# Long convolution by token residue modulo four, with part of its elementwise work on GpSimd

## The chip, the cores and the metric

One core of a Trainium2 chip runs the whole kernel, all in 32-bit floats. The metric is the device time of one execution in microseconds; the kernel before takes 4211.11 us (median of three runs, 4209.9 to 4212.46).

## What is computed

The reference is two transformer blocks over 1024 tokens of width 1024. The first block has a retention branch, a gated long convolution (the "hyena" branch) and a mixture of experts; the second has latent attention, a recurrent branch and another mixture of experts. Only the long convolution is touched. Cut to what matters:

```
zf = rfft(z, n=2048, axis=tokens)                       # z: 1024 tokens x 512 channels
hf = rfft(h_fwd, n=2048) + conj(rfft(h_bwd, n=2048))
y  = irfft(zf * hf, n=2048)[:1024] + z * skip
out = x0 * y                                            # x0, z, out: 1024 x 512
```

## The kernel before, in words

The program is a chain of phases. Each phase is a block with its own semaphores and one instruction list per engine, and the next phase begins on every engine only when all have left the last. SP issues most loads (the rows show its queue as SPq).

The transforms are products with tables of cosines and sines. Before the change the tokens are split into even and odd ones, 512 each, and a frequency and its mirror image share the work: with E the sum over even tokens and O the sum over odd ones, the two are E+O and E-O. So each table is 512x512, stored as 4 frequency tiles (`kt`) by 4 token tiles (`mt`) of 128x128. One product is 128x128 by 128 x 512 channels, 32-bit, and the trace shows it as two MATMUL records.

`phase_front` (L667) makes the two filters in K.X and loads frequency tiles 0 and 1 of the table `k_fwd` and the first tokens.

`phase_forward_norm` (L939) transforms the filters and at the same time normalises and transposes the tokens. VectorE first makes `he` and `ho`, the sum and the difference of the two filters (L1031, L1035). TensorE does 16 groups of four products, each followed by four 128x128 transposes of normalised tokens (L991, L998). ScalarE evicts half of the transposes (L1018) and the odd half of a pair of groups (L1023). VectorE evicts the other transposes (L1062) and forms H (L1068 to L1072).

`phase_taps` (L2005) projects, applies the short convolution and the gate, and transposes z into token order by residue (L2043, a source read at a step of two elements, 8 bytes). In its weight sums GpSimd works beside VectorE (L1936 to L1941). `Pairs` holds their code.

`phase_convolve` (L1075) does the convolution: for each of four frequency tiles 16 forward products (L1119), ScalarE's copies of the odd sums (L1148), and 20 VectorE operations of 128x512, each (L1156 to L1178): four butterflies, the complex product with H in two halves, four recombinations into K.X. Then come the inverse products (L1111), 64 in all, even tokens first, and for each of the 8 result banks VectorE adds the skip term (L1184) and multiplies with x0 (L1187), over every second token:

```
dve.scalar_tensor_tensor(odd[:, n % 2, :], split(xc[:, 4 + c, :], par), vec(K.cols, "hy_skip", c),
                         bk[n][:, :], ALU.mult, ALU.add).then_inc(skipped, 1)
dve.wait_ge(skipped, n + 1)
dve.tensor_tensor(split(hyT[:, c, :], par), odd[:, n % 2, :], split(xc[:, c, :], par), ALU.mult)
```

`Chain` issues an instruction and makes its engine wait until that one has finished. The order of every engine is written out by hand. The retention branch's first phase (`context`) follows.

Of the kernel before, what the change touches and what calls it, by code (L numbers as in the profile page):

```python
# [15 lines left out]
F32 = mybir.dt.float32  # L16
# [5 lines left out]
P = 128  # L22
D = 1024
KT = D // P
SEQ = 1024
# [630 lines left out]
def fwd_table(I, F, kt):  # L656

    return F.tab[:, kt % 2, :, :], I["k_fwd"][kt].rearrange("p (a n) -> p a n", n=P)
# [280 lines left out]
def phase_forward_norm(nc, I, K, fl, F, he, ho, H, src, outT, scale, shift):  # L939


    NT, XS, YS, FB = SEQ // P, 3, 3, 6
    with Mem(nc, "fwdnorm") as m:
        tab, x, full, xin = F.tab, F.x, F.full, F.xin
        odd = m.sb("odd", [P, 2, C])
        ys = m.sb("y", [P, YS, D])
        sq = m.sb("sq", [P, D])
        ss = m.sb("ss", [P, NT, 4])
        bk = m.banks(8)
        fb, nb = bk[0:FB], bk[FB:8]  # L950
        evac = m.sems("evac0", "evac1")
        hes, mm, copied, outs = m.sems("hes", "mm", "copied", "outs")
        summed, rooted, inv, yok, turned = m.sems("summed", "rooted", "inv", "yok", "turned")
        b = m.block()
        tok = lambda t: slice(t * P, (t + 1) * P)

        @b.sync
        def _(sp):
            def table(kt):

                if kt >= 2:
                    sp.wait_ge(mm, 4 * (kt - 1))
                sp.dma_start(tab[:, kt % 2, :, :], I["k_fwd"][kt].rearrange("p (a n) -> p a n", n=P)).then_inc(full[kt % 2], 16)

            def tokens(t):

                if t >= XS:
                    sp.wait_ge(yok, t - XS + 1)
                sp.dma_start(x[:, t % XS, :], src[tok(t), :]).then_inc(xin[t % XS], 16)

            tokens(3)
            tokens(4)
            table(2)
            tokens(5)
            tokens(6)
            table(3)
            tokens(7)

        @b.tensor
        def _(pe):  # L980
            for n in range(16):
                kt, a = divmod(n, 4)
                if a == 0:
                    pe.wait_ge(full[kt % 2], 16 * (kt // 2 + 1))
                if n >= FB:
                    pe.wait_ge(outs, (n - FB) // 2 + 1)
                part = (he, he, ho, ho)[a]
                if kt == 0:
                    pe.wait_ge(hes, 4 * (a + 1))
                for mt in range(4):  # L990
                    last = pe.matmul(fb[n % FB][:, :], tab[:, kt % 2, a * 4 + mt, :], part[:, (a % 2) * 4 + mt, :], start=(mt == 0), stop=(mt == 3))  # L991
                last.then_inc(mm, 1)
                t, h = divmod(n, 2)
                if h == 0:
                    pe.wait_ge(yok, t + 1)
                pe.wait_ge(evac[h], t + 1)
                for q in range(4):
                    last = pe.transpose(nb[h][:, q * P:(q + 1) * P], ys[:, t % YS, (4 * h + q) * P:(4 * h + q + 1) * P], K.ident[:, :])  # L998
                last.then_inc(turned, 1)

        @b.scalar
        def _(act):
# [12 lines left out]
            for t in range(NT):  # L1015
                act.wait_ge(turned, 2 * t + 1)
                for k in range(4):
                    last = act.activation(outT[:, k, tok(t)], nb[0][:, k * P:(k + 1) * P], ACT.Identity, scale=scale(k), bias=shift(k))  # L1018
                last.then_inc(evac[0], 1)
                act.wait_ge(mm, 2 * t + 2)  # L1020
                if t >= 2:
                    act.wait_ge(outs, t - 1)
                act.activation(odd[:, t % 2, :], fb[(2 * t + 1) % FB][:, :], ACT.Copy).then_inc(copied, 1)  # L1023
                if t + 2 < NT:
                    squares(t + 2)

        @b.vector
        def _(dve):
            def filt_he(t):

                dve.tensor_tensor(he[:, t, :], fl[:, t, 0:C], fl[:, t, C:2 * C], ALU.add).then_inc(hes, 1)  # L1031

            def filt_ho(t):

                dve.tensor_tensor(ho[:, t, :], fl[:, t, 0:C], fl[:, t, C:2 * C], ALU.subtract).then_inc(hes, 1)  # L1035
# [11 lines left out]
            for t in range(4):  # L1047
                filt_he(t)
            normed(0)
            for t in range(4, 8):  # L1050
                filt_he(t)
            normed(1)
            for t in range(4):
                filt_ho(t)
            for t in range(4, 8):
                filt_ho(t)
            for t in range(NT):
                if t + 2 < NT:
                    normed(t + 2)
                dve.wait_ge(turned, 2 * t + 2)  # L1060
                for k in range(4, 8):
                    last = dve.tensor_scalar(outT[:, k, tok(t)], nb[1][:, (k - 4) * P:(k - 3) * P], scale(k), shift(k), ALU.mult, ALU.add)  # L1062
                last.then_inc(evac[1], 1)
                kt, j = divmod(t, 2)
                dve.wait_ge(copied, t + 1)
                even = fb[2 * t % FB]
                if j == 0:
                    dve.tensor_tensor(H[:, kt, 0, :], even[:, :], odd[:, t % 2, :], ALU.add)  # L1068
                    dve.tensor_tensor(H[:, kt, 1, :], even[:, :], odd[:, t % 2, :], ALU.subtract).then_inc(outs, 1)
                else:  # L1070
                    dve.tensor_tensor(H[:, kt, 2, :], odd[:, t % 2, :], even[:, :], ALU.add)
                    dve.tensor_tensor(H[:, kt, 3, :], odd[:, t % 2, :], even[:, :], ALU.subtract).then_inc(outs, 1)  # L1072


def phase_convolve(nc, I, K, zn, H, prod, xc, hyT):  # L1075


    with Mem(nc, "conv") as m:
        tab = m.sb("tab", [P, 2, 16, P])
        odd = m.sb("odd", [P, 2, C])  # L1080
        z = m.sb("z", [P, 4, C])
        t = m.sb("t", [P, 4, C])
        y = hyT[:, :, 0:C]
        back = [[tab[:, a, :, :].rearrange("p (k b) n -> p k (b n)", b=4) for a in range(2)], [z[:, :, :], t[:, :, :]]]
        bk = m.banks(8)
        full = m.sems("full0", "full1")
        bfull = [m.sems("bfull00", "bfull01"), m.sems("bfull10", "bfull11")]
        mm, copied, outs, chain, turned, bmm, skipped = m.sems("mm", "copied", "outs", "chain", "turned", "bmm", "skipped")
        b = m.block()
        multiplied = lambda kt: 4 * (kt + 1)  # L1090

        @b.sync
        def _(sp):
            table = lambda par, a: I["k_inv"][par].rearrange("p (a n) -> p a n", n=C)[:, 4 * a:4 * a + 4, :]
            for kt in range(4):
                if kt >= 2:
                    sp.wait_ge(mm, 4 * (kt - 1))
                sp.dma_start(tab[:, kt % 2, :, :], I["k_fwd"][kt].rearrange("p (a n) -> p a n", n=P)).then_inc(full[kt % 2], 16)
            for a in range(2):
                sp.wait_ge(mm, 4 * (3 + a))  # L1100
                sp.dma_start(back[0][a], table(0, a)).then_inc(bfull[0][a], 16)
            sp.wait_ge(chain, multiplied(3))
            for a in range(2):
                sp.dma_start(back[1][a], table(1, a)).then_inc(bfull[1][a], 16)

        @b.tensor
        def _(pe):

            def inverse(par, c, a, kt, first, last):

                return pe.matmul(bk[4 * par + c][:, :], prod[:, kt, 2 * par + a, c * P:(c + 1) * P], back[par][a][:, kt, :], start=first, stop=last)  # L1111

            for kt in range(4):
                pe.wait_ge(full[kt % 2], 16 * (kt // 2 + 1))
                if kt >= 2:
                    pe.wait_ge(outs, kt - 1)
                for a in range(4):
                    for mt in range(4):
                        last = pe.matmul(bk[kt % 2 * 4 + a][:, :], tab[:, kt % 2, a * 4 + mt, :], zn[:, (a % 2) * 4 + mt, :],  # L1119
                                         start=(mt == 0), stop=(mt == 3))  # L1120
                    last.then_inc(mm, 1)
            pe.wait_ge(outs, 3)
            pe.wait_ge(chain, multiplied(2))
            for a in range(2):
                pe.wait_ge(bfull[0][a], 16)
                for c in range(4):
                    for kt in range(3):
                        inverse(0, c, a, kt, a == 0 and kt == 0, False)
            pe.wait_ge(chain, multiplied(3))
            for c in range(4):  # L1130
                inverse(0, c, 0, 3, False, False)
                inverse(0, c, 1, 3, False, True).then_inc(bmm, 1)
            for a in range(2):
                pe.wait_ge(bfull[1][a], 16)
            pe.wait_ge(outs, 4)
            for c in range(4):
                for n in range(8):
                    last = inverse(1, c, n // 4, n % 4, n == 0, n == 7)
                last.then_inc(bmm, 1)

        @b.scalar
        def _(act):
            for kt in range(4):
                for j in range(2):
                    act.wait_ge(mm, 4 * kt + (2 if j == 0 else 4))
                    if kt:
                        act.wait_ge(outs, kt)
# [2620 lines left out]
```

## Time and profile before

| | |
|---|---|
| median of three runs | 4211.11 us |
| span of the profiled execution, first to last instruction | 4218.0 us |
| TensorE busy | 3775.0 us, 89% |
| VectorE busy | 1511.3 us, 36% |
| ScalarE busy | 1024.2 us, 24% |
| GpSimd busy | 607.1 us, 14% |
| mean granted clock of TensorE | 0.961 of full speed |

The profile prints no other time of the profiled execution than its span, 6.9 us (0.16%) above the median. Times in rows count from the span's start. PE is TensorE's products, PEld its weight loads, DVE VectorE, ACT ScalarE, POOL GpSimd, SPq the DMA issues of SP. The arrow in brackets names what ended an idle time. A merged row ("x8") shows start and length of a run of equal instructions. The last record of a run of products overlaps the next instruction, so spacing is read from starts.

### The profile page before, as it was taken

The numbers are of one execution on the slowest core, as the hardware profiler recorded it, in microseconds if no ns is written. First come the engines' busy times: TensorE is split into PE (matmuls) and PEld (weight loads), VectorE is DVE, ScalarE is ACT, GpSimd is POOL, SyncE is SP. The second block draws the span as 40 slices with busy tenths as digits, with TensorE's granted clock in tenths as the row PEclk, the third lists the DMA queues.
The fourth block names the chain that finished last, engine by engine and source line by source line (L and its number), as shares of the span: only waits on it lengthen the run. The fifth ranks groups of instructions, "written<-read, shape, count | busy, mean of one in ns | idle before, by whom it ended". The sixth has DMA issues, their size and how long they took to land. (4 is left out here: it accounts for less than half of the span.)

```text
span 4218.0 us, 96770 instructions
## 1 busy us (share of the span) xinstructions
PE 3775.0 (89%) x42145; PEld 2433.0 (58%) x42145; DVE 1511.3 (36%) x2627; ACT 1024.2 (24%) x2394; POOL 607.1 (14%) x748
## 2 busy tenths in 40 slices
PE   7999899989999799999978999978888799996995
PEld 2444448864444488888854444457777544445774
DVE  5465235541212400000053666645556522222003
ACT  3201100131101122222242441034455211112333
POOL 1120000001000000000010001335555311000112
PEclk9999999999999799999989999989999999997998
DMA  8352332121112389999950001100000211306998
GB/s 296 131 166 80 131 90 80 60 55 35 35 35 104 148 337 389 394 394 397 400 186 15 9 2 45 45 2 4 4 4 4 78 35 52 101 35 244 385 386 313
DMA packets 243728, 601.68 MB, mean 143 GB/s; under 512 B 37593, under 2 KB 150008, under 8 KB 223515
## 3 DMA queue, kind: packets, MB, share of 16 engines
q1 hardware_dynamic: 200723, 471.21, 30.8%
q0 software_dynamic: 19120, 73.68, 5.1%
q10 hardware_dynamic: 23640, 53.20, 3.8%
q8 instruction: 194, 3.18, 0.3%
q14 instruction: 51, 0.42, 0.0%
HBM read 522.78 MB, written 71.05 MB: 141 GB/s over the span
## 5 line engine op out<-in xcount | busy, mean ns | idle before, releaser
L1752 PE MATMUL experts_bank<-experts_uT,ex_wu 128*64 128x96 f32 x9216 | 390.2, 247 | 26.9 <-PE experts_bank L1738 22.2
L1752 PEld LDWEIGHTS experts_bank<-experts_uT,ex_wu 128*64 128x64 f32 x9216 | 383.9, 137 | 43.6 <-issue 43.6
L1825 DVE TENSOR_TENSOR experts_hT<-experts_si,experts_bank 128x384 f32<-128x384 f32 (+1 forms) x68 | 31.3, 460 | 724.2 <-PE experts_bank L1752 724.2
L1752 PE MATMUL experts_bank<-experts_uT,b2z_hT 128*64 128x96 f32 x4096 | 178.4, 248 | 27.0 <-DMA b2z_hT<-in_w 17.8
L1752 PEld LDWEIGHTS experts_bank<-experts_uT,b2z_hT 128*64 128x64 f32 x4096 | 172.9, 138 | 41.6 <-issue 41.6
L1738 PE MATMUL experts_bank<-mixed_T,experts_hT 128*32 128x256 f32 (+1 forms) x2592 | 194.2, 451 | 0.0
L1738 PEld LDWEIGHTS experts_bank<-mixed_T,experts_hT 128*32 128x32 f32 x2592 | 111.1, 110 | 69.1
L1780 ACT ACTIVATE experts_uT<-experts_bank,all_modrun 128x96 f32<-128x96 f32 x296 | 99.3, 439 | 212.6 <-PE experts_bank L1733 212.6
L2401 POOL TENSOR_TENSOR b2z_hT<-b2z_hT,rwkv_level 128x256 f32<-128x256 f32 x192 | 140.8, 767 | 44.2 <-DVE b2z_hT L2880 34.0
L1361 DVE TENSOR_TENSOR merge_u<-merge_bank,merge_sg 128x512 f32<-128x512 f32 x16 | 11.1, 691 | 338.9 <-PE merge_bank L1294 338.9
L1718 POOL COPY experts_now<-ex_idx 96x1 int32 x68 | 12.5, 184 | 798.3 <-PE experts_bank L1733 788.5
L3282 PE MATMUL mh_sc<-mla_KTs,mh_QT 128*128 128x512 f32 x256 | 120.7, 594 | 5.9 <-ACT mla_KTs L3327 5.9
L1485 PE MATMUL route_bank<-ex_wu,mixed_T 128*128 128x512 f32 x256 | 114.3, 606 | 9.0 <-DMA ex_wu<-in_w_out 9.0
L1280 PE MATMUL merge_bank<-mix_qk,merge_w 128*128 128x512 f32 x256 | 114.9, 603 | 5.1 <-DMA merge_w<-in_ret_w_o 5.1
L2421 PE MATMUL rc_banks<-rc_xy,rc_p 64*64 64x64 f32 x2560 | 106.9, 220 | 8.3 <-issue 8.1
L485 PE MATMUL qk_bank<-mix_hT,all_X 128*128 128x512 f32 x256 | 110.1, 592 | 1.0 <-PEq L48 1.0
L3334 ACT ACTIVATE mh_pb<-mh_sc,mh_mx 128x1024 f32<-128x1024 f32 x64 | 71.3, 1114 | 152.6 <-DVE mh_mx L3367 152.6
L1832 DVE TENSOR_TENSOR experts_yo<-experts_bank,experts_gt 128x512 f32<-128x512 f32 x72 | 40.2, 558 | 183.7 <-PE experts_bank L1738 183.7
L2421 PEld LDWEIGHTS rc_banks<-rc_xy,rc_p 64*64 64x64 f32 x2560 | 91.8, 136 | 16.1 <-issue 15.7
L2421 PE MATMUL rc_banks<-rc_xy,b2z_hT 64*64 64x64 f32 x2560 | 80.8, 229 | 19.7 <-DVE rc_xy L2889 11.5
L1791 ACT ACT_TABLE_LOAD x34 | 43.6, 1283 | 222.3 <-PE experts_bank L1752 222.3
L1327 ACT ACTIVATE merge_sg<-merge_sg,all_cols 128x512 f32<-128x512 f32 x64 | 46.2, 721 | 202.8 <-DVE merge_sg L1367 84.0
(617 smaller groups left out, 7239.2 us busy)
## 6 DMA issues: line engine op xcount, KB each, us to landing
ex_wu<-in_expert_w SPq DMA_DIRECT2D x72, 2048.0 KB, 16.8
mixed_T<-in_expert_w SPq DMA_DIRECT2D x36, 2048.0 KB, 21.4
b2z_hT<-in_w SPq DMA_DIRECT2D x64, 1024.0 KB
b2z_Z<-in_w SPq DMA_DIRECT2D x32, 1024.0 KB, 13.5
keep_rows<-mix_hyT ACTq DMA_DIRECT2D x27, 768.0 KB, 8.7
keep_rows<-experts_yo ACTq DMA_DIRECT2D x68, 288.0 KB, 9.7
mix_hT<-in_ada_w POOLq DMA_DIRECT2D x8, 2048.0 KB, 13.3
vg_w<-in_w_in SPq DMA_DIRECT2D x32, 512.0 KB, 4.8
```

Of the source, the lines that this page charges most:

```text
L485: last = pe.matmul(bk[2 * (n % 2) + h][:, :], wt[:, n % 2, k, :], xT[:, k, hs[h]], start=(k == 0), stop=(k == KT - 1))
L1280: last = pe.matmul(bk[2 * j + h][:, :], w[:, s, k0 + k, :], at(x, k, slice(h * HALF, (h + 1) * HALF)), start=(k == 0), stop=(k == kn - 1))
L1327: act.activation(sg[:, g, h, :], sg[:, g, h, :], ACT.Sigmoid, bias=K.cols[:, bass.ds(i * 2 + (s + gate_col + 8 * g), 1)]).then_inc(sig, 1)
L1485: last = pe.matmul(mb[2 * (t % 2) + h][:, :], xT[:, k, tok(t)], wt[k // 2][:, k % 2, halves[h]], start=(k == 0), stop=(k == KT - 1))
L1738: return pe.matmul(bk[4 + 2 * s + j][32 * c:32 * c + 32, at:at + n], hT[:, k * BT + 32 * tokens:k * BT + 32 * tokens + 32], wd[:, s, k, c0 ...
L1752: last = pe.matmul(bk[2 + j][c:c + 64, h * BT:(h + 1) * BT], wu[:, s, j, k, h * P + c:h * P + c + 64], uT[:, s, k, :], start=(k == 0), sto ...
L1780: last = act.activation(uT[:, slot, k, :], bk[k // 4][:, k % 4 * BT:(k % 4 + 1) * BT], ACT.Identity, scale=scale(k), bias=shift(k) if shif ...
L1791: act.activation(si[:, :], bk[2][:, 0:HT * BT], ACT.Silu).then_inc(sil, 1)
L2401: gp.tensor_tensor(lev[d][:, l, :, :], arb[d][:, :, 0, :], W.level[:, d, l:l + 1, :].to_broadcast([P, J, CH]), ALU.mult).then_inc(pos[d], 1)
L2421: last = pe.matmul(out[heads[n ^ cross]], lhsT[hp], rhs[hp], start=start, stop=stop)
L3282: last = pe.matmul(sc[g % 2][:, half(x)], QT[:, h % 2, u * P:(u + 1) * P], KTs[:, h // 2 % 2 * 2 + h % 2, half(x)], start=True, stop=True)
L3334: act.activation(pb[:, g % 2, :], sc[g % 2][:, :], ACT.Exp, bias=mx[:, g % 2:g % 2 + 1], accum_out=sm[:, g % 2:g % 2 + 1]).then_inc(exped, 1)
```

## The change

Tokens are now split by residue modulo four, 256 each, and four frequencies share the work. A table is 256x256: 2 frequency tiles by 2 token tiles. `k_fwd` holds for each frequency tile ten such tables (cosine and sine of four residues, and two negated ones) and `k_inv` is one table of 2 MB.

- Filter transform: 8 groups. Even groups take 2 products per half, odd ones 4, so 48 instead of 64. The 64 transposes stay. `ho` is made by GpSimd. The negated tables are loaded at the phase's start into hyT. Every second group has no copy by ScalarE; VectorE handles it in two operations on 1024 columns.
- Taps: the transposes of z read at a step of four elements (16 bytes).
- Convolution: 32 forward products, 8 butterfly pairs (`level`, 16 operations of 512 columns from PSUM), then `spectrum`: 16 operations per frequency tile, 8 on 2 x n and 8 on 4 x n columns. VectorE does n = 384 channels, GpSimd the other 128, at the same time. The skip term is 8 products of a diagonal matrix with z (read at 16 bytes) into the result banks. 64 inverse products of 256 columns follow. The gate is 8 operations on PSUM that read and write at 16 bytes.

Core of the diff:

```diff
-            for t in range(4):
-                filt_ho(t)
-            for t in range(4, 8):
-                filt_ho(t)
+        @b.gpsimd
+        def _(gp):
+            for r in RES:
+                for t in (2 * r, 2 * r + 1):
+                    gp.tensor_tensor(ho[:, t, :], fl[:, t, 0:C], fl[:, t, C:2 * C], ALU.subtract).then_inc(hos, 1)
...
+        GROUPS = ((((COS[0], 0, 0),), ((COS[1], 0, 2),)),
+                  (((COS[2], 0, 1), (COS[3], 0, 3)), ((SIN[2], 0, 1), (NEG[1], 0, 3))),
+                  (((SIN[0], 1, 0),), ((SIN[1], 1, 2),)),
+                  (((SIN[2], 1, 1), (SIN[3], 1, 3)), ((COS[2], 1, 1), (NEG[0], 1, 3))))
...
+                if kt == 0:
+                    pe.wait_ge((hes, hes, hos, hos)[g], 2 * (h + 1) if g % 2 == 0 else 8)
...
-                        src = zc[:, 4 + c, :].rearrange("p (n two) -> p two n", two=2)[:, par, mt * P:(mt + 1) * P]
+                        src = residues(zc[:, 4 + c, :])[:, r, mt * P:(mt + 1) * P]
...
+        def spectrum(eng, then, kt, ch, between=lambda n: None):
+            first, z, t, y, w, out = [ap[:, :, ch] for ap in stages[kt]]
+            h = H[:, kt, :, ch]
+            eng.tensor_tensor(z[:, 0:2, :], first[:, 0:2, :], first[:, 2:4, :], ALU.add)
...
+            eng.tensor_tensor(t[:, 0:4, :], z[:, 0:4, :], h[:, 0:4, :], ALU.mult)
...
+            between(0)
+            eng.tensor_tensor(y[:, 0:4, :], t[:, 0:4, :], t[:, 4:8, :], ALU.subtract)
...
+            between(1)
+            eng.tensor_tensor(w[:, 0:5:4, :], y[:, 0:2, :], y[:, 2:4, :], ALU.add)
...
+            eng.tensor_tensor(out[:, 0:4, :], w[:, 0:4, :], w[:, 4:8, :], ALU.add)
+            return eng.tensor_tensor(out[:, 4:8, :], w[:, 0:4, :], w[:, 4:8, :], ALU.subtract)
...
+            for kt in range(2):
+                sp.dma_start(tab[:, kt, :, :], I["k_fwd"][kt].rearrange("p (a n) -> p a n", n=P)[:, 0:16, :]).then_inc(full[kt], 16)
+            sp.dma_start(back[:, :, :, :, :].rearrange("p r a k n -> p (r a k n)"), I["k_inv"]).then_inc(bfull, 16)
...
+            pe.wait_ge(diags, 4)
             for c in range(4):
+                pe.wait_ge(levelled, 4 + c + 1)
+                for x in range(2):
+                    pe.matmul(bk[2 * c + x][:, :].rearrange("p (r q) -> p r q", r=2), diag[:, c, :], every(4 + c)[:, 2 * x:2 * x + 2, :], start=True, stop=False)
+            pe.wait_ge(bfull, 16)
+            for kt in range(2):
+                pe.wait_ge(pmade, kt + 1)
+                inverse(kt, 3)
+                pe.wait_ge(dmade, kt + 1)
+                for c in range(3):
+                    inverse(kt, c)
...
+        @b.gpsimd
+        def _(gp):
+            then = Chain(gp, poold)
+            for kt in range(2):
+                gp.wait_ge(levelled, 4 * kt + 4)
+                if kt:
+                    gp.wait_ge(pmade, kt)
+                spectrum(gp, then, kt, slice(SPLIT, C)).then_inc(pmade, 1)
...
+            for g in range(4):
+                level(0, g)
+            dve.wait_ge(levelled, 4)
+            spectrum(dve, then, 0, slice(0, SPLIT), lambda n: [level(1, g) for g in (2 * n, 2 * n + 1)]).then_inc(dmade, 1)
+            dve.wait_ge(levelled, 8)
+            dve.wait_ge(dmade, 1)
+            spectrum(dve, then, 1, slice(0, SPLIT)).then_inc(dmade, 1)
```

`SPLIT` is 384. `inverse(kt, c)` does the 8 products of one frequency tile for one of four channel tiles; `every` is the view of a channel tile by residue.

## Rows read from the trace of the kernel before

**Rows 1.** Windows: length, busy us (count) of PE, PEld, DVE, ACT, POOL; clock; DMA.

```profile
93.50:163.50 70.00, 64.10 (x192) 31.39 (x192) 36.91 (x81) 28.83 (x65) 0.00 (x0) 0.95 0.19 68
...
323.40:442.20 118.80, 112.24 (x256) 49.27 (x256) 61.74 (x96) 4.78 (x8) 0.00 (x0) 0.97 0.20 71
```

**Rows 2.** Timeline, long convolution: start us, us, engine, line, count, idle before.

```profile
328.38 57.23 PE L1119 MATMUL conv_bank<-hy_xc,conv_tab 128*128 128x512 f32 x128 [6.11 <-DMA conv_tab<-in_k_fwd]
...
345.08 0.69 DVE L1156 TENSOR_TENSOR conv_z<-conv_bank,conv_odd 128x512 f32<-128x512 f32 x1 [21.88 <-ACT conv_odd L1148]
...
385.45 27.70 PE L1111 MATMUL conv_bank<-conv_tab,all_X 128*128 128x512 f32 x64
...
440.66 0.75 DVE L1184 SCALAR_TENSOR_TENSOR conv_odd<-hy_xc,all_cols,conv_bank 128x512 f32<-128x512 f32 x1 [5.39 <-PE conv_bank L1111]
441.44 0.69 DVE L1187 TENSOR_TENSOR mix_hyT<-conv_odd,hy_xc 128x512 f32<-128x512 f32 x1
```

**Rows 3.** Timeline of TensorE, one half step of the filter transform.

```profile
141.14 3.60 PE L991 MATMUL fwdnorm_bank<-hyf_ho,hyf_tab 128*128 128x512 f32 x8
144.57 0.60 PE L998 MATMUL fwdnorm_bank<-all_ident,fwdnorm_y 128*128 128x128 f32 x4
145.01 3.60 PE L991 MATMUL fwdnorm_bank<-hyf_he,hyf_tab 128*128 128x512 f32 x8
```

**Rows 4.** Timeline, beginning and end of the filter transform.

```profile
93.92 2.50 DVE L1031 TENSOR_TENSOR hyf_he<-all_X 128x512 f32<-128x512 f32 x4 [0.39 <-PEq L48]
...
96.56 5.57 PE L991 MATMUL fwdnorm_bank<-hyf_he,hyf_tab 128*128 128x512 f32 x8 [8.24 <-DVE hyf_he L1031]
...
100.14 0.75 DVE L1044 TENSOR_SCALAR fwdnorm_y<-hyf_x,fwdnorm_ss 128x1024 f32<-128x1024 f32 x1
...
160.70 1.36 DVE L1062 TENSOR_SCALAR mix_hT<-fwdnorm_bank,all_mod 128x128 f32<-128x128 f32 x4 [5.18 <-PE fwdnorm_bank L998]
...
162.58 0.68 DVE L1072 TENSOR_TENSOR hy_H<-fwdnorm_odd,fwdnorm_bank 128x512 f32<-128x512 f32 x1
```

**Rows 5.** Groups by shape on GpSimd: count, busy us, mean ns, idle before.

```profile
L2361 POOL TENSOR_TENSOR rc_bd<-rc_sa,all_X 128x256 f32<-128x256 f32 x32 | 22.6, 726 | 0.0
...
L1261 POOL TENSOR_TENSOR merge_ws<-merge_w 128x512 f32<-128x512 f32 x16 | 20.2, 1264 | 484.6 <-DMA merge_w<-in_w_in 484.6
```

**Rows 6.** Timeline, VectorE and GpSimd together, 170 to 176 us.

```profile
170.05 2.72 POOL L1936 TENSOR_TENSOR hin_ws<-hin_w 128x512 f32<-128x512 f32 x1 [5.05 <-DMA hin_w<-in_w_in]
...
171.57 3.35 DVE L1928 TENSOR_TENSOR all_X<-mix_hT,all_X 128x2048 f32<-128x2048 f32 x1
...
172.85 3.19 POOL L1938 TENSOR_TENSOR hin_ws<-hin_ws,hin_w 128x512 f32<-128x512 f32 x1
```

**Rows 7.** Timeline, VectorE and GpSimd together, 197 to 203 us.

```profile
197.13 0.75 DVE L1983 SCALAR_TENSOR_TENSOR hin_up<-hin_bank,all_cols,hin_u 128x512 f32<-128x512 f32 x1 [1.42 <-PE hin_bank L1946]
197.17 1.27 POOL L1936 TENSOR_TENSOR hin_ws<-hin_w 128x512 f32<-128x512 f32 x1 [18.56 <-PE hin_bank L1946]
...
200.19 2.13 POOL L1940 TENSOR_TENSOR hin_w<-hin_w 128x512 f32<-128x512 f32 x1
...
201.24 2.17 DVE L2076 SCALAR_TENSOR_TENSOR hy_xc<-hin_up,all_cols,hy_xc 128x1024 f32<-128x1024 f32 x1
```

**Rows 8.** DMA issues, 320 to 450 us: KB each, median us to landing.

```profile
conv_tab<-in_k_fwd SPq DMA_DIRECT2D x4, 1024.0 KB, 5.9
```

**Rows 9.** Lines 2043 and 1733, their weight loads: ns min/median/max.

```profile
L2043 PEld LDWEIGHTS hin_bank<-all_ident,hy_xc x32: 196/209/217, 318.2 to 321.9; 128*128 128x128 f32 x32
...
L1733 PEld LDWEIGHTS experts_bank<-all_ident,ex_xg x560: 185/206/231, 1471.2 to 4167.9; 96*128 96x128 f32 x187
```

**Rows 10.** Timeline of TensorE, values projection, 256 columns a product.

```profile
642.43 3.62 PE L215 MATMUL vgproj_bank<-vg_w,mix_hyT 128*128 128x256 f32 x16
645.88 3.62 PE L215 MATMUL vgproj_bank<-vgproj_ws,mix_hyT 128*128 128x256 f32 x16
```

**Rows 11.** Window at the start of the convolution's forward products.

```profile
328.40:332.60 4.20, 4.20 (x5) 1.83 (x6) 0.00 (x0) 0.00 (x0) 0.00 (x0) 0.51 0.41 172
```

More of the change, by code:

```diff
@@ L979, in _ @@
+            for t in range(3, NT):
+                sp.wait_ge(yok, t - XS + 1)
+                sp.dma_start(x[:, t % XS, :], src[tok(t), :]).then_inc(xin[t % XS], 16)
+        @b.gpsimd
[3 more added lines that the diff above has]
+                    gp.tensor_tensor(ho[:, t, :], fl[:, t, 0:C], fl[:, t, C:2 * C], ALU.subtract).then_inc(hos, 1)
         @b.tensor
         def _(pe):
[L981 to L999, printed above, removed]
@@ new lines, in _ @@
+            for j in range(8):
+                kt, g = divmod(j, 4)
+                if g == 0:
+                    pe.wait_ge(full[kt], 16)
+                if j == 1:
+                    pe.wait_ge(negs, 32)
+                if j >= SPARE:
+                    pe.wait_ge(outs, j - SPARE + 1)
+                for h in range(2):
+                    terms = GROUPS[g][h]
+                    if kt == 0:
+                        pe.wait_ge((hes, hes, hos, hos)[g], 2 * (h + 1) if g % 2 == 0 else 8)
+                    for n, (a, of, r) in enumerate(terms):
+                        for mt in range(2):
+                            last = pe.matmul(fb[j % SPARE][:, h, :], table(kt, a, mt), (he, ho)[of][:, r * 2 + mt, :],
+                                             start=(n == 0 and mt == 0), stop=(n == len(terms) - 1 and mt == 1))
+                    last.then_inc(mm, 1)
+                    if h == 0:
+                        pe.wait_ge(yok, j + 1)
+                    pe.wait_ge(evac[h], j + 1)
+                    for q in range(4):
+                        last = pe.transpose(nb[h][:, q * P:(q + 1) * P], ys[:, j % YS, (4 * h + q) * P:(4 * h + q + 1) * P], K.ident[:, :])
+                    last.then_inc(turned, 1)
@@ L1135, in _, with inverse @@
[L1135 to L1139, printed above, removed]
+            def inverse(kt, c):
+                for r in range(4):
+                    for a in range(2):
+                        last = pe.matmul(bk[2 * c + r // 2][:, r % 2 * 256:(r % 2 + 1) * 256], stages[kt][5][:, AT[r, a], c * P:(c + 1) * P],
+                                         back[:, r, a, kt, :], start=False, stop=(kt == 1 and a == 1 and r % 2 == 1))
+                    if kt == 1 and r % 2:
+                        last.then_inc(bmm, 1)
@@ L1179, in _, with level @@
-            split = lambda ap, par: ap.rearrange("p (n two) -> p two n", two=2)[:, par, :]
-            for par in range(2):
-                for c in range(4):
-                    n = par * 4 + c
-                    dve.wait_ge(bmm, n + 1)
-                    dve.scalar_tensor_tensor(odd[:, n % 2, :], split(xc[:, 4 + c, :], par), vec(K.cols, "hy_skip", c),
-                                             bk[n][:, :], ALU.mult, ALU.add).then_inc(skipped, 1)
-                    dve.wait_ge(skipped, n + 1)
-                    dve.tensor_tensor(split(hyT[:, c, :], par), odd[:, n % 2, :], split(xc[:, c, :], par), ALU.mult)
+            def level(kt, g):
+                n = 4 * kt + g
+                to, even, other = stages[kt][0], bk[2 * g], odd[:, n % 2, :]
+                dve.wait_ge(copied, n + 1)
+                plus, minus = ((0, 1), (2, 5), (6, 7), (4, 3))[g]
+                dve.tensor_tensor(to[:, plus, :], even[:, :], other, ALU.add)
+                if g == 2:
+                    dve.tensor_tensor(to[:, minus, :], other, even[:, :], ALU.subtract).then_inc(levelled, 1)
+                else:
+                    dve.tensor_tensor(to[:, minus, :], even[:, :], other, ALU.subtract).then_inc(levelled, 1)
```

260 lines of the change are left out of this document (119 added, 141 removed).

## The prediction

> **What bounds the kernel now.** I read the windows first, by stage. In the filter transform TensorE is busy 64.10 of 70.00 us, in the convolution 112.24 of 118.80 us, and GpSimd 0.00 us in both; VectorE has 36.91 and 61.74 us [rows 1]. Over both, then, TensorE is the bound, and the other engines wait for it. The timeline of the convolution says the same piece by piece: VectorE's first butterfly comes after 21.88 us without work, its last gate after 5.39 us of waiting for TensorE's last bank [rows 2]. Since all engines meet between phases, what one of these two phases becomes shorter by, the whole becomes shorter by. The question is only what ends last in each when TensorE has less to do.
>
> **Filter transform.** Half a step is four products, 3.43 us from 141.14 to 144.57, and four transposes, 0.44 us [rows 3]. So a product costs 0.86 us. 16 of 64 go: 16 x 0.86 = 13.7 us less on TensorE. What stands beside it:
>
> The start. Before, VectorE made four parts of `he` in 2.50 us, 0.62 us each, and TensorE started at 96.56 [rows 4]. Now GpSimd subtracts at the same time. How the two behave together is in two stretches. GpSimd's operation of 170.05 ran 2.72 us, and its next one, started 172.85, 3.19 us; alone the same shape takes 1.26 [rows 5]. VectorE's of 171.57 ran 3.35 us. The ends fit only one way: GpSimd waited until VectorE's next operation was issued at 171.57, ran to 172.77 while VectorE stood, then VectorE ran to 174.92 while GpSimd stood, then GpSimd to 176.04 [rows 6]. They exclude each other, operation by operation, in turns. The second stretch gives the prices in turns: VectorE's operation before that of 201.24 ended at about 201.2; from there to 202.32, 1.12 us, GpSimd does its 512 columns, and from there to 203.41, 1.09 us, VectorE its 1024 [rows 7]. It also shows what is exempt: the VectorE operation at 197.13, which reads one operand from PSUM and one from SBUF, keeps 0.75 us beside GpSimd's 1.27 [rows 7].
>
> At the start every VectorE operation has its inputs in SBUF, so the 8 of `he` (0.55 us in turns) alternate with the 8 of `ho` (1.12 us). The two normalisations (0.75 us [rows 4]) stand fifth and tenth in VectorE's order and take turns too. From 93.92: first two parts at 96.2, as before; fourth 99.6; first normalised tokens 101.2; eighth part 107.9, where before it was at 100.0. TensorE's group 1 needs all eight, so it starts at 107.9. Left are 44 products, 37.7 us, and 14 sets of transposes, 6.1 us, with 1 us for a start at low clock: end 152.7. The group pairs need 12 us of TensorE and less than 9 of VectorE or ScalarE, so nothing else is late. The new tables, 512 KB asked for at 94, are not needed before 104: a load of 1 MB takes 5.9 us [rows 8], so the load is covered.
>
> The end. Before, VectorE started the last eviction at 160.70 and ended at 163.26 [rows 4]. The last group now has two operations of 1024 columns instead of two of 512: 1 us more. So 152.7 + 0.2 + 1.3 + 2.3 = 156.5, a gain of 6.8 us. If the engines did not take turns: 13.7 - 1.0 = 12.7. If TensorE's pause also cost a full low-clock start, 4.9.
>
> **Taps.** The transposes read their source at 16 bytes a step instead of 8. No row has 16; one has 32: line 1733, 206 ns a weight load against 209 ns at 8 bytes on line 2043 [rows 9]. So I put 0; bounds -0.1 and +0.3 us over 32.
>
> Here the Trainium skill speaks against the change. "SBUF — State Buffer", in "Door 1: The DMA port swizzle", says that 16 bytes form a line, and that each access in a new line pays a penalty. Row and rule differ for the weight operand, where 32 bytes a step cost nothing, and the row decides. For the streamed operand (the diagonal products) and for VectorE's gate no row has such a step; the rule would make them slower, by an amount it does not give.
>
> **Convolution.** *Forward.* The first frequency tile is 16 products as before, so its last copy is at hand at 345.08 as before [rows 2]. Before, VectorE had nothing until then; now three of four butterfly pairs are done by then, and the fourth takes 2 x 0.62: 346.3. TensorE goes on with the second tile, 13.7 us, to about 358, and ends 27 us before the old 385.45 [rows 2].
>
> *Spectrum.* It starts at 346.3 on both engines, all inputs in SBUF. VectorE per tile: 8 operations of 768 columns and 8 of 1536. By 1.09 us for 1024 [rows 7] these are 0.82 and 1.62 us, 19.5 us. GpSimd per tile: 8 of 512 (1.12) and 8 of 256. Alone they are 1.26 and 0.73 us [rows 5]; 0.14 of it is not in turns, so 0.58, and 13.6 us. Both tiles: 39.0 and 27.2 us. VectorE also has the second tile's butterflies in between, 8 x 0.6 = 4.8 us; these read PSUM, and GpSimd gets 4 operations done under them, 3.4 us. The last four operations of VectorE meet no GpSimd operation any more, another 3.4 us not waited for. VectorE ends at 346.3 + 39.0 + 4.8 + (27.2 - 3.4 - 3.4) = 410.5, plus about 4 us: eight waits of `Chain` kind (0.12 each), the start part of operations out of turn, and turns in which GpSimd takes two for one. I take 414.5. The last term is a choice; without it 410.5, with all of GpSimd's work in VectorE's way 417.3.
>
> *Inverse.* A product of 256 columns takes 3.45 us / 8 = 0.43 us [rows 10]. The first tile's 32 come in the gap while the second spectrum runs, and the diagonal products (8 x 0.86 = 6.9 us, or 13.7 if the step doubled them) before those, between 358 and about 380; both are covered. After GpSimd's last come 8 products, 3.4 us, begun at low clock: in the window after a pause the granted clock is 0.51, 1.2 GHz, for 4.2 us [rows 11], so 2.1 us lost, still before 414.5. Then 24 products: 10.3 us, to 424.8, and one gate of 0.7: 425.5. Before it ended at 442.13 [rows 2], so the gain is 16.6 us. That the old inverse was 55 us and the new 27 counts little: it is the 10 us behind the last spectrum that count. The gate operations, 0.7 us, stay under TensorE's 1.7 us a bank even if the step doubled them; the last would cost 0.6 us more. The skip operation goes with the diagonal products, and so does 0.75 us of the tail (in the sum).
>
> *Loads.* First, two tables of 1 MB, as before; behind them 2 MB for the inverse, not needed before 370. If the three shared the DMA engines instead of following one another, the first table would land up to 5 us later. I put 0, since 5.9 us a table [rows 8], with two asked for together, is a queue's order.
>
> **Sum.** 6.8 + 0 + 16.6 = 23.4 us. The profiled execution spans 4218.0 and would span 4194.6; the median of the runs lies 6.9 us lower, so 4211.1 - 23.4 = 4187.7, -0.56%.
>
> The Trainium skill ("SBUF — State Buffer", "Who interferes with whom") has the exclusion as a rule: a VectorE instruction with two SBUF inputs and a GpSimd one that reads SBUF block each other for a whole instruction. By it the sum is the above, and the trace agrees; the next case is what the split promises if it did not hold.
>
> **The rivals.**
> - *True sharing.* The two engines run side by side in `spectrum`, three quarters and a quarter. Then VectorE's tile is 20.5 us, its end 346.3 + 41 + 4.8 + 1 = 393.1, the phase's end 404, gain 38; with 12.7 in the filter transform 51 us: 4160. For it: GpSimd's operations here are shorter than in the stretches shown, and have gaps. Against it: every overlap of operations that read only SBUF [rows 6, 7]. 10%.
> - *Turns cost more than the bare times.* The place is the hand-over of the port, 64 in the two spectra (32 operations on either side) and 16 at the filter's start, 80. The gain of 23.4 us is gone at 0.29 us each; at 0.5 us the kernel takes 4211.1 + 16.6 = 4228. Against it: VectorE's 1.09 us for 1024 columns in turns is next to half of the 2.15 for 2048 [rows 6], so the hand-over is within 0.02 us there. For it: no row has a long alternation of unchained small operations. 5%.
> - *A step of 16 bytes, or the loads, cost on the path.* First table 5 us late, low clock for the last 24 products (2.1), a doubled last gate (0.6), low end of the filter transform (1.9): 9.6 us less gain, 4197. With twice that in the tables and strided reads, 4207, the same as before within the noise. For it: no row has such a step on a streamed operand. 20% for 4193 to 4203, 6% beyond.
>
> **How the numbers follow.** Forecast with its own range 4180 to 4193: 59%. True sharing 4155 to 4180: 10%. The third rival 26%, turns 5%. About 0.2% (8.4 us) is what a measurement of this kernel tells from no change. Faster than 4202.7: 0.59 + 0.10 + 0.20 = 0.89; within: 0.06; slower: 0.05. The range 4170 to 4203 leaves out 8% of sharing and 11% above, and holds the price ends: 410.5 and 417.3 for the spectrum, 4.9 and 12.7 for the filter.
>
> **What would show each step.** In the profile after: GpSimd's operations of 512 columns in the convolution well over 1.26 us in the mean and VectorE's of 1536 well over 1.7, both near 2.5 (right), or at 1.26 and 1.7 (true sharing). TensorE idle between about 390 and 405. The filter transform's group 1 starting about 11 us after the first, not 5. The convolution 102 us from its first load to its last gate, not 119. The forecast is wrong if the spectra together last under 55 us or over 75, or if phases outside these two change by more than 2 us.

## The result, and the profile after

The changed kernel takes 4186.85 us in the median of 4 runs (4185.6 to 4192.48), the kernel before in the same runs 4210.9 us (4 runs, 4209.9 to 4212.46). The ratio is 0.9943, 95% interval 0.9929 to 0.9957, or 0.57% faster. The forecast was 4187.7 us. The profiled execution spans 4183.8 us where the one before spans 4218.0.

The windows of the changed kernel's two stages, and of shorter stretches in them; the columns are those of [rows 1]:

```profile
92.50:158.50 66.00, 53.55 (x160) 26.08 (x160) 44.81 (x72) 26.47 (x61) 13.24 (x9) 0.89 0.15 48
316.90:419.50 102.60, 74.64 (x208) 42.74 (x208) 80.78 (x56) 5.94 (x12) 61.32 (x32) 0.85 0.10 41
...
107.10:111.10 4.00, 4.00 (x5) 1.78 (x6) 3.96 (x9) 0.00 (x0) 0.00 (x0) 0.50 0.53 159
...
385.90:401.60 15.70, 0.00 (x0) 0.00 (x0) 15.60 (x8) 0.00 (x0) 15.54 (x8) 0.62 0.00 0
401.70:405.90 4.20, 4.20 (x10) 3.39 (x11) 4.17 (x4) 0.00 (x0) 0.00 (x0) 0.50 0.00 0
406.00:418.00 12.00, 12.00 (x55) 10.36 (x53) 8.33 (x8) 0.00 (x0) 0.00 (x0) 0.97 0.00 0
```

In the convolution TensorE fell from 112.24 busy us [rows 1] to 74.64. VectorE, 80.78, and GpSimd, 61.32, now show 142 us between them in a stage of 102.6: an overlap in the records, of which the experiments will show that little is work done side by side. For 15.7 us TensorE does nothing at all while both others have records throughout.

The filter transform in the timeline of the changed kernel (start us, us, engine, line, count, idle before), against [rows 4]:

```profile
92.79 12.98 POOL L988 TENSOR_TENSOR hyf_ho<-all_X 128x512 f32<-128x512 f32 x8 [22.16 <-POOLq L48]
92.80 6.82 DVE L1048 TENSOR_TENSOR hyf_he<-all_X 128x512 f32<-128x512 f32 x4 [0.39 <-PEq L48]
96.42 3.52 PE L1006 MATMUL fwdnorm_pair<-hyf_he,hyf_tab 128*128 128x512 f32 x4 [9.06 <-DVE hyf_he L1048]
...
99.73 1.56 DVE L1057 TENSOR_SCALAR fwdnorm_y<-hyf_x,fwdnorm_ss 128x1024 f32<-128x1024 f32 x1
101.21 5.71 DVE L1048 TENSOR_TENSOR hyf_he<-all_X 128x512 f32<-128x512 f32 x4
...
156.74 1.21 DVE L1091 TENSOR_TENSOR hy_H<-fwdnorm_pair,mix_hyT 128x1024 f32<-128x1024 f32 x1
```

Four `he` parts take 6.82 us instead of 2.50 [rows 4], and a normalisation 1.56 instead of 0.75. The stage lasts from 92.80 to 157.95, 65.2 us, where it was 69.3: a gain of 4.2 us.

The convolution in the timeline of the changed kernel, against [rows 2]:

```profile
316.97 0.82 SPq L1140 DMA_DIRECT2D conv_tab<-in_k_fwd  x2
...
339.31 0.96 DVE L1118 TENSOR_TENSOR all_X<-mix_hyT 128x768 f32<-128x768 f32 x1
...
349.44 2.71 DVE L1124 TENSOR_TENSOR hy_H<-all_X,hy_H 128x1536 f32<-128x1536 f32 x1
350.61 2.66 POOL L1124 TENSOR_TENSOR hy_H<-all_X,hy_H 128x512 f32<-128x512 f32 x1
...
356.35 14.73 PE L1167 MATMUL conv_bank<-hy_xc,conv_tab 128*128 128x512 f32 x16 [5.30 <-DVE all_X L1210]
...
399.63 1.97 POOL L1135 TENSOR_TENSOR hy_H<-all_X 128x512 f32<-128x512 f32 x1
...
401.66 16.60 PE L1150 MATMUL conv_bank<-conv_back,hy_H 128*128 128x256 f32 x64 [15.86 <-POOL hy_H L1135]
...
405.00 1.75 DVE L1135 TENSOR_TENSOR hy_H<-all_X 128x1536 f32<-128x1536 f32 x1
...
418.29 1.05 DVE L1224 TENSOR_TENSOR mix_hyT<-conv_bank,hy_xc 128x512 f32<-128x512 f32 x1 [0.65 <-PE conv_bank L1150]
```

From its first load to its last gate the convolution takes 102.4 us (316.97 to 419.34) against 118.7 (323.46 to 442.13 before): 16.3 us gained. The idle time of the row at 401.66, 15.86 us until GpSimd's last operation, is the stage's new wait. The ends of the two rows at 349.44 and 350.61 show one turn: VectorE's operation ended at 352.15, and GpSimd's, whose record began while VectorE's ran, at 353.27, 1.12 us later, the price of a turn in [rows 7].

The two profiled spans differ by 34.2 us, the medians by 24. The convolution ends 22.8 us earlier: 4.2 and 16.3 by the two stages, 1.1 because the filter transform began earlier, and 1.2 between the stages. The other 11.4 us lie behind it, in phases that the change doesn't touch. Nearly half, 5.3 us, comes by the experts' first product: 1033.6 us from the convolution's end before (442.13 to 1475.7), 1028.3 after (419.34 to 1447.6); but two more executions of the changed kernel took 1029.1 and 1034.2 there, so a single execution varies by as much. Another 2.5 us are in the experts' first part, 637.4 us before and 634.9, 634.9 and 635.0 in three executions after; what they are stays open. So stages are compared below, each by one profiled execution, and totals only where several runs were timed. How much a stage varies by itself shows in five profiled executions with the changed convolution as it is (the changed kernel's three, e2 and e7): 102.4 to 103.4 us.

### The profile page after: what moved, and what is told of

Read it like the earlier page. It is cut to its first block and busy times, and to the rows that moved or that the text cites. A ratio compares the mean times of both kernels' runs of the same rounds, so it can differ in the third digit from the quotient of the medians.

```text
span 4183.8 us, 96598 instructions
## 1 busy us (share of the span) xinstructions
PE 3721.8 (89%) x42065; PEld 2418.4 (58%) x42065; DVE 1539.6 (37%) x2579; ACT 1024.2 (24%) x2394; POOL 679.4 (16%) x788
## 5 line engine op out<-in xcount | busy, mean ns | idle before, releaser
L2459 PE MATMUL rc_banks<-rc_xy,rc_p 64*64 64x64 f32 x2560 | 106.5, 220 | 10.2 <-issue 10.1
L1299 POOL TENSOR_TENSOR merge_ws<-merge_w 128x512 f32<-128x512 f32 x16 | 20.2, 1264 | 484.8 <-DMA merge_w<-in_w_in 484.8
```

Of the source, the lines that this page charges most:

```text
L2459: last = pe.matmul(out[heads[n ^ cross]], lhsT[hp], rhs[hp], start=start, stop=stop)
```

## The experiments

My theory is that of the forecast: operations of VectorE and GpSimd that read only SBUF go in turns, so GpSimd's share is added to VectorE's time and not taken from it. The rivals: GpSimd's share helps; or the 16-byte steps, the low clock or the waits cost the time. Each run is compared with the changed kernel timed in the same set (a1_after for e1, e2 and e4, a2_after for e3, e5 and e6; e7 has none beside it). e3, e6 and e7 were run once. Except in the last kernel, each edit touches one of the two stages.

**The changed kernel again (a1_after).**

> The changed kernel as it is, to be compared with its variants on the same chip. Filter transform 65 us, convolution 102 us from first load to last gate, 0.994 of the kernel before.

It took 4197.84 us against 4219.44 (ratio 0.9947, 0.9932 to 0.9962). The convolution takes 103.4 us, the filter transform 62.1 instead of 65.2. The windows of this execution show where the 3 us are:

```profile
95.20:109.40 14.20, 6.20 (x16) 2.76 (x17) 14.13 (x12) 7.39 (x15) 12.91 (x8) 0.77 0.23 74
109.40:113.00 3.60, 3.59 (x9) 1.64 (x10) 3.56 (x9) 0.00 (x0) 0.00 (x0) 1.00 0.51 154
```

After nearly the same start as in the first execution (TensorE busy for 6.20 us of 14.20, the last 2.91 of them without work; there 6.33) group 1's first eight records run at a granted clock of 1.00, 2.4 GHz, and take 3.67 us. In the first execution they began at 0.50, 1.2 GHz, and took 6.7.

**No GpSimd in the spectra (e1_dve_all).**

```diff
-    SPLIT = 3 * P
+    SPLIT = C
...
-                pe.wait_ge(pmade, kt + 1)
-                inverse(kt, 3)
                 pe.wait_ge(dmade, kt + 1)
-                for c in range(3):
+                for c in range(4):
                     inverse(kt, c)
...
-        @b.gpsimd
-        def _(gp):
...
-            dve.wait_ge(pmade, 2)
-            for n, c in enumerate((3, 0, 1, 2)):
+            for n, c in enumerate((0, 1, 2, 3)):
```

> VectorE does all 512 channels of both spectra, GpSimd none. Turns (the two engines exclude each other): the operations become 1.14 us (1024 columns) and 2.2 us (2048), 26.7 us a tile, none waits for the other engine; VectorE ends 8 us earlier, TensorE then has 32 products left instead of 24 (13.8 us and 2 us of low clock), so the convolution is about 98 us instead of 102 and the kernel 4 us faster than the changed one. True sharing (GpSimd's quarter was free): VectorE's 62 us of spectrum become a third longer, the convolution about 127 us, the kernel 25 us slower than the changed one.

4201.0 us, ratio to before 0.9955 (0.994 to 0.997). The median is 3.2 us above a1_after's, where 4 us below was expected; the ranges overlap and no difference can be told. The convolution takes 100.1 us (322.43 to 422.52), 3.3 less than the 103.4 of a1_after with GpSimd's help, and 2.3 less than the shortest of the changed kernel's; 4 were expected. The timeline:

```profile
349.91 2.29 DVE L1122 TENSOR_TENSOR mix_hyT<-all_X,hy_H 128x2048 f32<-128x2048 f32 x1
...
405.00 16.43 PE L1150 MATMUL conv_bank<-conv_back,hy_H 128*128 128x256 f32 x64 [10.95 <-DVE hy_H L1135]
```

VectorE does all four quarters in 2.29 us an operation; with GpSimd's help its three quarters mostly took 2.2 to 2.9. Its spectra go from 345.25 to 404.94, 59.7 us against 67.4. That only 3.3 of these 7.7 us reach the end is the order of the inverse: GpSimd's quarter let TensorE begin its first 16 records 5.1 us before VectorE's end, and here all 64 come after VectorE.

**The filter's differences on VectorE (e2_ho_dve).**

```diff
-        @b.gpsimd
-        def _(gp):
-            for r in RES:
-                for t in (2 * r, 2 * r + 1):
-                    gp.tensor_tensor(ho[:, t, :], fl[:, t, 0:C], fl[:, t, C:2 * C], ALU.subtract).then_inc(hos, 1)
...
             normed(1)
+            for r in RES:
+                for t in (2 * r, 2 * r + 1):
+                    dve.tensor_tensor(ho[:, t, :], fl[:, t, 0:C], fl[:, t, C:2 * C], ALU.subtract).then_inc(hos, 1)
```

> ho is made by VectorE, after the second normalisation as before the change; nothing else differs. Turns: the eight parts of he are there 6 us earlier, TensorE's group 1 starts without the 2.9 us pause and without a second low-clock start; filter transform about 59 us instead of 65, kernel 6 us faster than the changed one. Rival (the negated tables or TensorE's own order set the pause, GpSimd is innocent): filter transform 65 us or, with 5 us more on VectorE, 70.

4194.99 us, ratio 0.994 (0.9925 to 0.9955), 2.9 us below a1_after where 6 were expected; the total alone does not tell the two apart, the stage does: 55.3 us (92.93 to 148.19) against 62.1. About 59 against 65 were expected. The timeline:

```profile
92.93 2.50 DVE L1042 TENSOR_TENSOR hyf_he<-all_X 128x512 f32<-128x512 f32 x4 [1.50 <-PEq L48]
...
99.81 4.89 DVE L1062 TENSOR_TENSOR hyf_ho<-all_X 128x512 f32<-128x512 f32 x8
...
100.44 3.60 PE L1000 MATMUL fwdnorm_pair<-hyf_he,hyf_tab 128*128 128x512 f32 x8
```

Group 1 starts 7.5 us after the stage's start, not 14.3, without a pause and at 3.60 us for eight records, the full clock's time [rows 3]. In a1_after it ran at full clock too, so group 1's clock has no part in these 6.8 us. VectorE makes all eight `ho` parts in 4.89 us, while TensorE has work.

**GpSimd's part only later (e7_ho_late).** It tells whether the engine or the moment cost.

```diff
         def _(gp):
+            gp.wait_ge(hes, 8)
             for r in RES:
```

> The changed kernel, but GpSimd begins its half of the filter transform's butterflies (ho, 8 operations of 512 columns) only after VectorE has done all of its he parts and so not while VectorE works on them. My theory: VectorE's he parts, which took 6.8 us for four beside GpSimd, go back to about 2.5 us for four as in the kernel before, the first group of products starts about 11 us after the stage's start instead of 14, and the filter transform takes 55 to 60 us like the kernel with no GpSimd work there (55.3 and 56.1 us), against 62.1 and 65.1 us, if the ho parts come before they are wanted. The rival: it is late ho parts, not VectorE's slowed ones, that cost; then the stage is as long as in the changed kernel or longer (62 to 70 us), since ho comes later still.

4180.72 us, one run, against one of the kernel before at 4206.84. The stage takes 56.4 us (94.07 to 150.48), and group 1 starts 8.7 us after its start; 11 were expected. The timeline:

```profile
94.07 2.50 DVE L1049 TENSOR_TENSOR hyf_he<-all_X 128x512 f32<-128x512 f32 x4 [0.39 <-PEq L48]
...
100.26 10.78 POOL L989 TENSOR_TENSOR hyf_ho<-all_X 128x512 f32<-128x512 f32 x8 [28.17 <-DVE hyf_he L1049]
100.28 1.79 DVE L1058 TENSOR_SCALAR fwdnorm_y<-hyf_x,fwdnorm_ss 128x1024 f32<-128x1024 f32 x1
...
102.72 3.60 PE L1007 MATMUL fwdnorm_pair<-hyf_he,hyf_tab 128*128 128x512 f32 x8
```

GpSimd's work is all there, 10.78 us of it, and the stage is as long as with none of it (55.3 us, and 56.1 in e5_vector_only). So it was the moment: VectorE's eight parts were on the path, and GpSimd's turns stood between them. The rival, late `ho`, is refuted.

**Half the columns on GpSimd (e4_split256).**

```diff
-    SPLIT = 3 * P
+    SPLIT = 2 * P
```

with TensorE's and the gates' order following it (GpSimd's two quarters first).

> GpSimd does half of the channels instead of a quarter. Turns: GpSimd costs 2.1 ns a column and VectorE 1.05, so each channel moved to GpSimd lengthens the common time: two tiles 79 us instead of 66, convolution 115 to 120 us, kernel 13 to 17 us slower than the changed one. True sharing: GpSimd's 2 x 27 us and VectorE's 2 x 14 side by side, at most as long as now: convolution 90 to 102 us.

4216.74 us, ratio to before 0.9999 (0.9988 to 1.001): the whole gain is gone. The median is 18.9 us above a1_after's, where 13 to 17 were expected. The convolution takes 117.5 us (317.45 to 434.98), 14.1 more. The timeline:

```profile
351.59 3.25 DVE L1124 TENSOR_TENSOR hy_H<-all_X,hy_H 128x1024 f32<-128x1024 f32 x1
...
353.83 3.20 POOL L1124 TENSOR_TENSOR hy_H<-all_X,hy_H 128x1024 f32<-128x1024 f32 x1
...
417.83 16.06 PE L1150 MATMUL conv_bank<-conv_back,hy_H 128*128 128x256 f32 x64 [22.51 <-POOL hy_H L1135]
```

VectorE has a third less to do in each operation and needs longer for it, 3.25 us instead of 2.71: it waits for an operation of GpSimd twice as long.

**GpSimd's quarter left out (e3_no_pool_share).** The spectrum of the last 128 channels is not computed; VectorE's three quarters are as in the changed kernel. TensorE and the gates take the four channel tiles in order, as in e1_dve_all, so all of TensorE's last 64 records come after VectorE. Only the convolution is read, since what the experts do later depends on the data.

```diff
-        @b.gpsimd
-        def _(gp):
-            then = Chain(gp, poold)
-            for kt in range(2):
-                gp.wait_ge(levelled, 4 * kt + 4)
-                if kt:
-                    gp.wait_ge(pmade, kt)
-                spectrum(gp, then, kt, slice(SPLIT, C)).then_inc(pmade, 1)
```

> GpSimd's quarter of the two spectra is left out, nobody does it (channels 384 to 511 of the convolution are not computed, which also changes what the experts get, so only the length of the convolution is read). Turns: VectorE's operations fall to 0.87 and 1.66 us from start to start, its last ends 46 us after the fourth butterfly pair instead of 67; convolution about 86 us. True sharing: VectorE's operations and end unchanged, since GpSimd was never in its way: 103 to 107 us.

```profile
341.65 0.96 DVE L1118 TENSOR_TENSOR all_X<-mix_hyT 128x768 f32<-128x768 f32 x1
...
348.71 1.76 DVE L1124 TENSOR_TENSOR hy_H<-all_X,hy_H 128x1536 f32<-128x1536 f32 x1
...
386.81 1.75 DVE L1135 TENSOR_TENSOR hy_H<-all_X 128x1536 f32<-128x1536 f32 x1
```

In this timeline VectorE's same operation takes 1.76 us, 2.71 beside GpSimd. Its spectra last 46.9 us (341.65 to 388.56) against 67.4, and the convolution 86.2 us (319.29 to 405.44). The spectra and the convolution, 47 and 86 us, came out as expected. So GpSimd's quarter stands in VectorE's time with 20.5 us; done on VectorE in e1_dve_all it took 59.7 - 46.9 = 12.8.

**Views without the residue step (e6_contiguous).** The skip's operand and the gate's are read and written in contiguous pieces, which are other tokens; only the durations are read.

```diff
-        every = lambda c: residues(xc[:, c, :])
+        every = lambda c: xc[:, c, :].rearrange("p (four q) -> p four q", four=4)
...
-                    dve.tensor_tensor(residues(hyT[:, c, :])[:, 2 * x:2 * x + 2, :],
+                    dve.tensor_tensor(hyT[:, c, :].rearrange("p (four q) -> p four q", four=4)[:, 2 * x:2 * x + 2, :],
```

> The diagonal products and the gate read and write in one piece instead of every fourth element (the same bytes in another token order, so the output's tokens are mixed up; only durations are read). If the 16-byte step costs: a diagonal product's record falls from 0.90 to 0.43 us from start to start and the gate from 1.08 to 0.69 us, the convolution by 0.4 us only, since the rest is under other work. If something else made them slow, both stay.

Its timeline:

```profile
355.49 5.19 PE L1167 MATMUL conv_bank<-hy_xc,conv_tab 128*128 128x512 f32 x8 [5.31 <-DVE all_X L1210]
...
362.32 3.70 PE L1167 MATMUL conv_bank<-hy_xc,conv_tab 128*128 128x512 f32 x8 [1.64 <-DVE all_X L1208]
...
417.55 0.69 DVE L1224 TENSOR_TENSOR mix_hyT<-conv_bank,hy_xc 128x512 f32<-128x512 f32 x1 [1.03 <-PE conv_bank L1150]
```

The diagonal products take 5.19 and 3.70 us for eight records (granted clock 0.70 and 1.00), together 8.9 against 14.73 with the step. A gate takes 0.69 us against 1.08. The diagonal products are hidden: the convolution takes 102.7 us, within what the changed kernel takes (102.4 to 103.4). From TensorE's start on the last products to the last gate's end it is 17.6 us against 18.0 in a1_after, which is the last gate's 0.4.

**The changed kernel beside the second set (a2_after).**

> The changed kernel again, beside the next variants on the same chip: 0.994 to 0.995 of the kernel before.

4199.92 us, ratio 0.9949 (0.9937 to 0.9961). Convolution 103.4 us again, filter transform 65.1, with group 1 at low clock; its window:

```profile
111.50:118.00 6.50, 6.50 (x9) 2.62 (x10) 3.95 (x9) 0.00 (x0) 0.00 (x0) 0.54 0.54 164
```

**Both stages without GpSimd, the inverse in step with VectorE (e5_vector_only).** The edits of e2_ho_dve and e1_dve_all, and VectorE makes the second tile's spectrum in two pieces, so that TensorE can start on the first:

```diff
-            spectrum(dve, then, 1, slice(0, SPLIT)).then_inc(dmade, 1)
-            dve.wait_ge(dmade, 2)
-            dve.wait_ge(pmade, 2)
+            spectrum(dve, then, 1, slice(0, 3 * P)).then_inc(dmade, 1)
+            spectrum(dve, then, 1, slice(3 * P, C)).then_inc(dmade, 1)
+            dve.wait_ge(dmade, 3)
...
                 for c in range(3):
                     inverse(kt, c)
+                if kt:
+                    pe.wait_ge(dmade, 3)
+                inverse(kt, 3)
```

> Both products of the split undone: VectorE makes ho, and does all channels of both spectra; the second tile's spectrum is done in two pieces, 384 channels and then 128, so that TensorE's last products of three channel tiles run under VectorE's last piece. Turns: filter transform 55 to 59 us instead of 62 to 65; convolution 93 us instead of 103 (VectorE's last piece ends 84 us after the first load, eight products and a gate follow); kernel about 17 us faster than the changed one, 0.990 of the kernel before. True sharing: convolution 120 us and more, the kernel slower than the changed one by 15 us.

4185.38 us (4181.32 to 4189.45), ratio to before 0.992 (0.9908 to 0.9933), 14.5 us below a2_after's median in the same rounds. The filter transform takes 56.1 us, the convolution 93.3 (310.26 to 403.53). The timeline:

```profile
386.35 16.09 PE L1147 MATMUL conv_bank<-conv_back,hy_H 128*128 128x256 f32 x64 [5.29 <-DVE hy_H L1132]
...
393.73 0.69 DVE L1132 TENSOR_TENSOR hy_H<-all_X 128x512 f32<-128x512 f32 x1
394.45 6.03 DVE L1213 TENSOR_TENSOR mix_hyT<-conv_bank,hy_xc 128x512 f32<-128x512 f32 x6
```

TensorE starts 8 us before VectorE's last spectrum operation ends, and 16.1 us of inverse and 1.1 of gate end the stage. By the stages it is 9.0 + 10.1 = 19.1 us below a2_after; about 17 were expected, and the medians show 14.5. The difference is no more than the phases behind vary by (1028.3 to 1034.2 us above). This version is faster than the kernel before by 0.8%, and its slowest run (4189.45) is below a2_after's fastest (4192.15).

## Why the prediction was right, and where its terms were off

The time, 4187.7 against 4186.85 us, and the mechanism held: TensorE now waits for `he` at the start of the filter transform and for the spectra in the convolution, and GpSimd's share is added to VectorE's time. That the total is within 1 us is luck. The measured stage gains were 4.2 + 16.3 = 20.5 us, the forecast's 6.8 + 16.6 = 23.4, and the phases behind made up the rest; in the repeats the medians are 21.6 and 17.5 us apart. Of the prediction's own signs, the convolution (102 us), group 1's start (10.7 us after the first group's, 11 forecast), TensorE's idle stretch (15.7 us, 15 forecast), the means of GpSimd's operations of 512 columns and VectorE's of 1536 (2.2 and 2.4 us, near 2.5 forecast) and the spectra's length (67.4, between 55 and 75) came as said. One sign of being wrong came too: a phase outside the two changed by more than 2 us, the experts' first part by 2.5. The forecast has no term for it, and no run explains it.

- *Turns, not sharing.* On record was VectorE's end 410.5 with a choice of 4 us upon it. From the first load: start of the spectrum 22.8 forecast, 22.3 measured; end 91.0 forecast, 89.8 measured. The terms in between are less good than that. VectorE's own part was put at 39.0 + 4.8 = 43.8 and is 46.9 in e3_no_pool_share: a piece of 768 columns takes 0.87 us start to start, not 0.82, one of 1536 takes 1.68, not 1.62, and waits come on top. GpSimd's net addition was put at 27.2 - 3.4 - 3.4 = 20.4 us, and the runs give 20.5, but the agreement is chance. The two deductions are one: four of GpSimd's operations done under the butterflies are the reason why VectorE's last four meet none. In the trace five of the 32 run mainly under the butterflies (one of 512 columns, four of 256) and 27 stand in VectorE's way. At the forecast's prices these are 15 x 1.12 + 12 x 0.58 = 23.8 us, and the net is 20.5. So the turns were priced 3.3 us too high, VectorE's own part 3.1 too low, and the 4 us of allowance, named for other things, made good the 3.4 that had been taken off twice.
- *The tail.* Forecast 10.3 + 0.7 us after VectorE's end, measured 12.6 (406.75 to 419.34). Of the 1.6 us more, 0.4 is the gate's step. Some 0.75 comes from a step of the prediction that its own numbers don't carry. It had GpSimd's eight products done before VectorE's end; but GpSimd ends four operations earlier, 4.9 us, and the products were put at 3.4 + 2.1 = 5.5. In the trace TensorE began at 401.66 at granted clock 0.50, 5.1 us before VectorE's end; nine of its 64 records were done at 406.0, and at 0.22 us a record the sixteenth ended at about 407.5, after VectorE. The stage's end hangs on GpSimd's last operation as much as on VectorE's.
- *Filter transform.* Group 1 was put 14.0 us after the stage's start and came after 14.3. The stage was to end at 156.5 from a start at 93.92, so 62.6 us long; it was 65.2, 62.1 and 65.1 in three executions. The mis-sized term is the low clock after the pause: put at 1 us, it was 3 us in two of three and nothing in the third. Four variants (e1, e3, e4, e6) leave this stage as it is; with them, in seven executions, group 1's eight records took 3.67 to 6.74 us and the stage 62.1 to 65.2, longer by just what the records took more. The bound of 4.9 us gain named it; the measured 4.2 lies a little below. That the pause was there at all is GpSimd's doing (e2_ho_dve, e7_ho_late).
- *Rivals.* True sharing is refuted by e1_dve_all and e4_split256: giving GpSimd twice as much costs 14.1 us in the stage, giving it nothing gains 2.3 to 3.3, where sharing promised a loss of 25. Turns that cost more than the bare times: no; 20.5 us against 23.8 at the bare prices leaves nothing for hand-overs. The 16-byte step and the loads: the step does double the diagonal products against contiguous ones at full clock, but they lie where TensorE waits anyway; its price on the path is 0.4 us. The third load moved nothing on the path: TensorE's first product came 4.9 us after the first load in the profiled execution before and in the one after.
- *Taps.* The weight loads at a 16-byte step have a median of 212 ns, against 209 [rows 9], as put.

```profile
L2081 PEld LDWEIGHTS hin_bank<-all_ident,hy_xc x32: 197/212/218, 311.7 to 315.4; 128*128 128x128 f32 x32
```

So the gain comes from TensorE's fewer products (37.6 busy us less in the convolution, 10.6 in the filter transform, by the windows), and it is given back in part: in the convolution the new wait is for the spectra, in the filter transform for `he`, and in both GpSimd's turns lengthen it. Without them, in e5_vector_only, the same transforms gain 69.3 - 56.1 = 13.2 and 118.7 - 93.3 = 25.4 us by the stages, 38.6 together. Its median lies 32.1 us below the one before; where the other 6.5 us go was not settled.

The Trainium skill ("SBUF — State Buffer", "Who interferes with whom") lists also VectorE's tensor-scalar operation among those that can lock the shared port; the normalisation's 1.79 us beside GpSimd against 0.75 alone (e7_ho_late) agrees.

## What to carry to other kernels

Here GpSimd was no second VectorE for work whose inputs all lie in SBUF: price its share as an addition to VectorE's time, at GpSimd's slower rate, and give it such work only where VectorE's part is not on the path. Before splitting work over engines, split it in time: a piece handed over early to the engine that waits shortened the convolution from 100.1 to 93.3 us (e1_dve_all, e5_vector_only), while a quarter done elsewhere lengthened it. After a change has taken work from the bounding engine, look at which piece it now waits for, and at what clock it wakes.

## What the runs showed of the hardware

- A streamed fp32 operand at a 16-byte step: 14.73 us for 16 records of 512 columns, 0.92 us each. Contiguous, eight take 3.70 us in e6_contiguous and 3.60 in [rows 3], 0.46 and 0.45 each. With the step TensorE's clock made next to no difference: the 16 records took 14.61 us at a granted clock of 1.00 (e3_no_pool_share), 14.61 at 0.88 (e1_dve_all) and 14.73 at 0.79 (the first execution), while eight contiguous ones took 3.70 at 1.00 and 5.19 at 0.70. The weight operand costs nothing more at that step (212 ns against 209), and VectorE's gate, which reads one operand and writes at it, takes 1.08 us instead of 0.69. The Trainium skill ("SBUF — State Buffer", "Door 1: The DMA port swizzle") speaks of a penalty for each access that goes to a new 16-byte line; the trace agrees for the streamed operand and the gate and gives the size, and differs for the weight load.
- After 14 us of the same instructions (6.33 and 6.20 us busy) and a pause of 2.91 us, TensorE's next records began at a granted clock of 0.50 in one execution and ran at 1.00 in another of the same kernel.
- 512 columns more on GpSimd add 0.95 us to the record of VectorE's operation beside them (2.71 - 1.76 us, 1536 columns); as part of VectorE's own operation they add 0.53 (2.29 - 1.76).
